# Streaming encoder step: projecting the Fox keys first, row tile by row tile

## The reference

```
h   = RMSNorm(x) @ W_in     # split into fq, fk, fv, forget | x, y | bq, bk, bv
mix = [fox_attention(fq, fk, fv, forget) | rglru(x, y) | band_attention(bq, bk, bv)] @ W_out
x   = x + RMSNorm(mix)
x   = x + RMSNorm(gated MLP with causal convolution(RMSNorm(x)))
```

## Time and profile before

| | us |
|---|---|
| three runs, median (lowest to highest) | 1543.34 (1542.04 to 1546.4) |
| the profiled execution | 1543.2 |
| its span | 1541.5 |
| PE busy, share of the span | 1461.6, 95% |
| DVE, ACT, POOL busy | 728.2, 458.4, 90.7 |
| chain that ended last, share of PE | 89% |

### The profile page before, as it was taken

One profiled execution on the slowest core, in us unless ns is written; L12 is line 12 of the kernel. 1 busy time (PEld: TensorE's weight loads), 2 busy tenths in 40 slices (PEclk: granted clock), 3 DMA queues, 4 the chain that ended last, 5 costly groups with the idle time before them and its releaser, 6 DMA issues.

```text
span 1541.5 us, 20612 instructions
## 1 busy us (share of the span) xinstructions
PE 1461.6 (95%) x8470; PEld 1325.3 (86%) x8470; DVE 728.2 (47%) x1216; ACT 458.4 (30%) x671; POOL 90.7 (6%) x129
## 2 busy tenths in 40 slices
PE   6999999978888899999999999999999999999994
PEld 6999979855666688989898989898989999999993
DVE  6433621166667555553536353535353535444336
ACT  6353332054446543412121212121212221212123
POOL 3000003211000002000000000000000000000006
PEclk9999999989999999999999999999999999999998
DMA  6210212225021323311010111101010101111033
GB/s 206 83 31 35 97 58 108 87 70 190 15 83 55 124 86 106 98 54 55 28 54 27 54 43 39 54 27 54 27 54 27 54 27 54 36 46 52 16 116 135
DMA packets 80005, 102.87 MB, mean 67 GB/s; under 512 B 3592, under 2 KB 63237, under 8 KB 79806
## 3 DMA queue, kind: packets, MB, share of 16 engines
q1 hardware_dynamic: 71744, 73.43, 15.4%
q0 software_dynamic: 8208, 28.69, 5.4%
HBM read 85.52 MB, written 16.58 MB: 66 GB/s over the span
## 4 chain that ended last, share of the span: by engine, by line
PE 89%; DVE 6%; ACT 2%; issue 1%; DMA 1%; POOL 0%; SPq 0%; ACTq 0%; DVEq 0%
PE PS L1423 49%; PE PS L1743 18%; PE PS L1492 7%; PE PS L1710 6%; PE PS L1413 3%; PE PS L1559 2%; PE PS L1665 1%; PE PS L1652 1%; DVE f_acc L1396 1%; DVE probs L1209 1%; PE PS L1498 1%; DVE kt_s L1186 1%; DVE f_acc L1369 1%; PE PS L1582 0%; DMA x_in<-in_x_prompt 0%
## 5 line engine op out<-in xcount | busy, mean ns | idle before, releaser
L1423 PE MATMUL PS<-act_hi,w_hi 128*128 128x384 f32 x1152 | 208.4, 334 | 0.0
L1423 PE MATMUL PS<-act_hi,w_lo 128*128 128x384 f32 x1152 | 207.9, 334 | 0.0
L1423 PE MATMUL PS<-act_lo,w_hi 128*128 128x384 f32 x1152 | 207.9, 334 | 0.0
L1423 PEld LDWEIGHTS PS<-act_hi,w_hi 128*128 128x128 f32 x1152 | 200.8, 188 | 0.9
L1423 PEld LDWEIGHTS PS<-act_hi,w_lo 128*128 128x128 f32 x1152 | 200.4, 188 | 0.0
L1423 PEld LDWEIGHTS PS<-act_lo,w_hi 128*128 128x128 f32 x1152 | 200.4, 188 | 0.0
L1369 DVE TENSOR_TENSOR f_acc<-f_acc,PS 128x512 f32<-128x512 f32 x216 | 145.5, 686 | 77.8 <-PE PS L1743 77.8
L1743 PE MATMUL PS<-w_hi,f_hi 128*128 128x512 f32 x432 | 168.8, 391 | 5.4 <-ACT ffn_rows L977 5.4
L1743 PE MATMUL PS<-w_hi,f_lo 128*128 128x512 f32 x432 | 168.4, 390 | 0.0
L1743 PE MATMUL PS<-w_lo,f_hi 128*128 128x512 f32 x432 | 168.3, 390 | 0.0
L899 ACT ACTIVATE w_hi<-raw 128x1024 fp32r<-128x1024 f32 x72 | 72.1, 1049 | 225.2 <-PE PS L1743 219.5
(11 more groups left out here) (326 smaller groups left out, 2002.9 us busy)
## 6 DMA issues: line engine op xcount, KB each, us to landing
raw<-in_w_up SPq DMA_DIRECT2D x48, 512.0 KB, 4.7
raw<-in_w_down SPq DMA_DIRECT2D x24, 512.0 KB, 3.9
raw<-in_w_in SPq DMA_DIRECT2D x18, 512.0 KB, 4.6
x_scratch<-x POOLq DMA_DIRECT2D x9, 512.0 KB, 5.0
x_back<-x_scratch SPq DMA_DIRECT2D x1, 4608.0 KB, 14.2
x_in<-in_x_prompt SPq DMA_DIRECT2D x8, 512.0 KB, 5.9
raw<-in_w_out SPq DMA_DIRECT2D x8, 512.0 KB, 3.6
x_res<-in_x_prompt SPq DMA_DIRECT2D x8, 512.0 KB, 4.1
```

The source lines that it names most:

```text
L1423: last = pe.matmul(PS[0:width, banks + c, 0:CW], w(wp, k), acts[ap][:, k, c * CW:(c + 1) * CW], start=(n == 0 and k == 0), stop=(n == 2 an ...
```

## The change

The Fox keys become unit 0. TensorE projects them tile by tile (`fk_tile`), 24 matmuls each, between the turns, into four PSUM banks by turns, and ScalarE copies each tile to `stage` (`take_fk`). Both weight halves of unit 0 are loaded and split ahead of row tile 1 instead of among tiles 2 and 3. x0 and x1 become ordinary outputs. The second gates stay behind y3, where fv0 to fv2 now follow; the third gates stand behind fv2, the fourth behind bv1. VectorE splits unit 5 after the first scan, units 6 and 7 after the second, 8 after the third, 9 after the fourth.

```diff
-UNITS = [("x", C_X), ("x", C_X + 256), ("y", C_Y), ("y", C_Y + 256), ("fk", C_FK), ("fv", C_FV),
+UNITS = [("fk", C_FK), ("x", C_X), ("x", C_X + 256), ("y", C_Y), ("y", C_Y + 256), ("fv", C_FV),
          ("bk", C_BK), ("bv", C_BV), ("fq", C_FQ), ("bq", C_BQ)]
...
-GATES_AFTER = [("y", 2, 0), ("y", 3, 3), ("fk", 4, 2), ("fv", 5, 2)]
+GATES_AFTER = [("y", 3, 0), ("y", 4, 3), ("fv", 5, 2), ("bv", 7, 1)]
...
-            for t in range(3):
-                sp.dma_start(x_in[:, t, :], rows_of(xp, xs, t)).then_inc(x_loaded[t], 16)
-                if t == 0:
-                    sp.dma_start(gains[:, 0, :], i["norm_g"][0, 0:1, :].to_broadcast([P, D]))\
-                      .then_inc(gain_loaded, 16)
+            sp.dma_start(x_in[:, 0, :], rows_of(xp, xs, 0)).then_inc(x_loaded[0], 16)
+            sp.dma_start(gains[:, 0, :], i["norm_g"][0, 0:1, :].to_broadcast([P, D])).then_inc(gain_loaded, 16)
...
             load_in(0)
             load_in(1)
-            for t in range(3, NT):
-                sp.wait_ge(y_ready, t - 2)
+            for t in range(1, NT):
+                if t >= 3:
+                    sp.wait_ge(y_ready, t - 2)
                 sp.dma_start(x_in[:, t % 3, :], rows_of(xp, xs, t)).then_inc(x_loaded[t % 3], 16)
...
+            def take_fk(t):
+
+                j, c = divmod(t, 3)
+                if j == 2 and c == 0:
+                    act.wait_ge(stage_stored[0], 16 * stores_until(0, 0))
+                if c < 2:
+                    act.wait_ge(fk_done, 2 * j + c + 1)
+                else:
+                    act.wait_ge(out_done, j + 1)
+                act.activation(stage[:, j % 2, c, :], PS[:, t % 4, 0:DH], ACT.Copy)\
+                   .then_inc(fk_used if c < 2 else out_used, 1)
...
+                if t == 0:
+                    for half in range(2):
+                        split_unit_half(0, half)
                 if t >= 1:
                     norm_hi(t - 1)
-                if t in FIRST_SPLITS:
-                    split_unit_half(0, FIRST_SPLITS.index(t))
+                if t >= 3:
+                    take_fk(t - 3)
             norm_hi(NT - 1)
+            for t in range(NT - 3, NT):
+                take_fk(t)
...
             for j in range(LT):
                 lru_scan(j)
                 if j < LT - 1:
-                    split_unit(5 + j)
+                    for u in ((5,), (6, 7), (8,))[j]:
+                        split_unit(u)
                     lru_conv(j + 1)
-            for u in range(8, NU):
-                split_unit(u)
+            split_unit(9)
...
+            def fk_tile(t):
                 pe.wait_ge(w_lo_ready, 2)
-                pe.wait_ge(lo_ready, 3 * (c + 1))
+                pe.wait_ge(lo_ready, t + 1)
+                if t >= 4:
+                    wait_fk_used(pe, t - 4)
                 w0 = [unit_of(w, 0) for w in (w_hi_all, w_lo_all)]
...
+                for m, (ap, wp) in enumerate(((0, 0), (0, 1), (1, 0))):
+                    for k in range(KD):
+                        last = pe.matmul(bank_cols(t % 4, DH), acts[ap][:, k, t * P:(t + 1) * P], w0[wp][:, k, :],
+                                         start=(m == 0 and k == 0), stop=(m == 2 and k == KD - 1))
+                last.then_inc(fk_done if t % 3 < 2 else out_done, 1)
+
+            turn_x(0)
+            turn_x(1)
+            for t in range(NT):
+                fk_tile(t)
+                if t + 2 < NT:
+                    turn_x(t + 2)
```

## The result

The changed kernel takes 1550.97 us (median of 6 runs, 1546.23 to 1552.3) against 1542.69 us of the kernel before on the same chip (6 runs, 1540.97 to 1546.4): ratio 1.0048, 95% interval 1.003 to 1.0065. It is slower, by 4.6 to 10.0 us by that interval. The forecast was 1548.9. In a second session six more runs gave 1551.76 (ratio 1.0062, 1.005 to 1.0075).

A forecast was written before the change was run, and what follows sets the result against it. TensorE, busy 95% of the span, bounds the kernel through its matmuls and queue holes. Front −3.4, clock +1.8, fv2 hole +5.5, clock +1.8 make +5.7 on 1543.2: 1548.9 us; 8-in-10 range 1542.5 to 1553.5.

The forecast's parts named there:

- Front: Start to x2: x1 lands later, key tiles and turns then run without a hole; net gain 3.4 us.
- rival 3: Front: turn, act_hi, act_lo and next y_in form one chain, 4.4 us per tile, not 3.78; +4.3 us, chance 0.10.
- Hole behind the keys: Before x0: TensorE waits 3.2 us for unit 1's split, queued behind the last key copy; counted within the 3.4 gain.
- Clock behind that hole: After the wait before x0: TensorE falls to half clock, 1.8 us lost, priced from the earlier 2.7 us hole.
- Rival 2: Before x0 and at fv2: both holes occur but the clock does not fall; 3.6 us less, 1545.3, chance 0.15.
- Hole at fv2: Before fv2: ScalarE awaits unit 7's halves before copying fv0, so TensorE stands 5.5 us for PSUM banks.
- rival 1: At fv2: no hole, ScalarE copies fv0 before fv1 ends; 1541.6 us, not slower, chance 0.12.
- rival 4: Before x0 and at fv2: both holes covered, only the front's gain left; 1536.6 us, faster, chance 0.06.
- Clock behind it: After the wait at fv2: TensorE's clock falls again, 1.8 us lost.
- Third gates: Behind fv2: no wait, convolution done 1.9 us early; without the fv2 hole, 3.6 of its 5.5 us would stay.
- Sum: Whole kernel: −3.4 + 1.8 + 5.5 + 1.8 = +5.7 us on 1543.2, giving 1548.9.

The follow-up runs named there:

- with filler: Changed kernel with 17 matmuls ahead of x0 and 29 ahead of fv2, results overwritten, order otherwise kept: 1544.97 us, ratio 1.0012.
- two shifted executions of the kernel before: Kernel before with 31 and with 16 matmuls, results overwritten, added ahead of fq0 on TensorE: 1549.76 and 1546.25 us.
- 16 fillers: Kernel before with 16 matmuls (2.8 us), results overwritten, added ahead of fq0 on TensorE: 1546.25 us, ratio 1.0026.
- 31 fillers: Kernel before with 31 matmuls (5.4 us), results overwritten, added ahead of fq0 on TensorE: 1549.76 us, ratio 1.0041.

## Why the prediction was right, and what it missed

- **Front.** x1 landed at 11.26 (11.7 in the prediction), the second turn started at 14.33 (14.7). The first key tile took 4.26 us (2.9 + 1.0 = 3.9), the others 2.87 (2.91). The keys end at 49.64 (50.0). Each step came within 0.5 us, the early landing and the slower first tile nearly cancel, and no key tile waits for `act_lo`, so rival 3, a slower front, is out.
- **Hole behind the keys.** 3.2 us by the waits (3.2), x0 at 53.53 (53.9). The step that makes it is shown by taking it away: with unit 1's split two copies earlier it is gone.
- **Clock behind that hole.** 24 matmuls in 5.96 us where the same row takes 4.40 at full clock, with filler: 1.6 (1.8). Rival 2, no fall of the clock, is out here: 53 to 57 us reads 0.57, and with filler 1.00. But the forecast drew its price from one row, the 2.7 us hole before, and that row is not the same in each execution: two others of the same front show no fall behind it. The new hole of 3.25 us was followed by half clock in all five profiled executions that have it without filler, at 1.6 to 2.8 us (5.96 to 7.24 instead of 4.40).
- **Hole at fv2.** 5.33 us (5.5). From the first low part to the start of the split that its transfer releases: low parts 177.56 to 179.91, so the first ends at about 178.7, and the split starts at 182.76: 4.0 us (3.9). The second ends at 179.94 by the chain, and its split starts at 184.75: 4.8 (4.9). So rival 1 is out, as is rival 4. By the fit of the Trainium skill, "DMA: Bandwidth & Descriptors", section on the anatomy of one DMA, given for transfers that GpSimd issues, 512 KB would be an estimated 3.2 us; both transfers here are longer, so the measured rows of the queue were the better price.
- **Clock behind it.** 4.64 − 3.02 = 1.6 (1.8); in the three other executions with a hole of 5.2 to 5.5 us there, 1.6 to 2.1.
- **Third gates.** No wait in the changed kernel, as worked out, and without the hole 3.7 us of it come back as a wait for the convolution (3.6). This figure was a side remark of the prediction and is one of its best tests.
- **Sum.** The marker moved by 5.37 us (5.7). Up to the marker the prediction was right in mechanism and size. That the two numbers lie so close is in part luck: 5.37 compares one execution with one. In the two shifted executions of the kernel before the marker, less the filler, lies at 300.8 and 300.7, which makes 6.5 and 6.6 of the 5.37.

What it missed is the rest: 8.3 us in the medians against 5.4 to 6.6 at the marker, so some 2 to 3 us that no term of the sum held. In the two profiled executions 2.8 of them lie in the attention stage, whose program is the same. The sum assumed that a shift passes through it unchanged. It does not from the first product on: that one costs the changed kernel 1.7 us more (3.65 against 1.97). But the kernel before loses as much in the matmuls that follow, up to 331 us, and at the wait for `kt_b`, of 1.63 us in both, the shift is 5.2 us again. From there it grows and stays. Before:

```profile
358.23 0.23 PE L1552 MATMUL PS<-cmask_b,ident_b 128*128 128x128 bf16 x1 [1.63 <-DVE kt_b L1192]
358.39 1.56 PE L1559 MATMUL PS<-kt_f,mix 64*128 64x512 f32 x8
359.88 0.87 PE L1413 MATMUL PS<-ident,probs 128*128 128x128 f32 x6
```

After:

```profile
363.44 0.23 PE L1577 MATMUL PS<-cmask_b,ident_b 128*128 128x128 bf16 x1 [1.63 <-DVE kt_b L1220]
363.60 2.50 PE L1584 MATMUL PS<-kt_f,mix 64*128 64x512 f32 x8
366.03 1.54 PE L1441 MATMUL PS<-ident,probs 128*128 128x128 f32 x6
```

Same wait, 5.2 us later; before, the next eight matmuls run at full speed, after, they and the turns behind them take 2.50 + 1.54 instead of 1.56 + 0.87: 1.6 us lost. Another 1.3 are lost in the same way behind the next wait for `kt_b`: four products and the six turns behind them run from 364.79 to 366.44 before, from 371.65 to 374.58 after. The granted clock agrees: from 50 to 70 us behind the marker it reads 1.00 in the kernel before and with 16 fillers, and 0.83 with 31 fillers and in all three executions of the changed kernel, shifted or not.

So the missing term, where the profile shows it, is TensorE's clock in a stage full of short waits: which of them are followed by 1.2 GHz differs from kernel to kernel. A shift alone can bring such a loss at the same place, as the kernel before with 31 fillers shows (2.0 of the 2.9 us). That the shift is the whole cause of the changed kernel's loss is not shown: there its size differs, and the gain ahead of the wait is missing. What decides, wait by wait, whether the clock falls stays open. The distance from the start does not sort it: the filler version of the changed kernel reaches the end of its wait for `kt_b` at 359.25 and takes 1.65 us for the four products behind the next one, the kernel before with 16 fillers at 359.55 and 0.92.

## What to carry to other kernels

On an engine that works through its queue in order, a step that waits for a transfer must not stand ahead of the copy that frees another engine's PSUM banks, as the split of unit 7 did. And a step whose result that other engine needs next must not stand behind a copy that waits for its last product, as the split of unit 1 did, whose weights had been there. Moving the two turned 0.5% slower into 0.5% faster. When such a hole is closed, look at what it covered: behind this one stood a convolution that was late as well, and half a repair gave back 3.7 of 5.3 us. A hole of 3.2 to 5.5 us in a dense row of matmuls cost its length and then 1.6 to 2.8 us of half clock in this kernel. A price read from one execution is weak: look at the same row in a second one.

## What the runs showed of the hardware

One and the same attention program took 211.9 to 215.6 us in the twelve profiled executions of these kernels. Where its parts differ in the rows compared here, matmuls behind the same short waits ran at another clock. Such a fall need not repeat: the same wait of 2.7 us in the front of the kernel before was followed by half clock in one execution (0.50 from 43 to 44 us) and by full clock in two. Twice the changed kernel gave nearly the same stage (215.6 and 215.4), which is too few to say that its place in the range is fixed. Matmuls with results that nobody reads, put into a hole, kept the granted clock at 1.00 behind it where it had read 0.57 and 0.79.
